# Softmax attention of the second block: nine projection units by seven block products each, their sums on VectorE

## What is computed

```python
def chunk_attention(u, w_in, b_in, rel_bias, w_out):
    q, k, v = jnp.split(u @ w_in + b_in, 3, axis=-1)     # u 256x1024, w_in 1024x3072
    ...                                                   # 16 heads of 64
        s = jnp.einsum('bhtd,bhjd->bhtj', qi, kb).astype(jnp.float32) + bias
        p = jax.nn.softmax(jnp.where(mb, s, NEG_INF), axis=-1).astype(vb.dtype)
        return jnp.einsum('bhtj,bhjd->bhtd', p, vb)
    ...
    return o @ w_out
...
    x = layer_norm_2(DEEPNORM_ALPHA * x + (1.0 + g1) * y, ln_g[i, 0], ln_b[i, 0])
```

## Time and profile before

| what | value |
|---|---|
| median of 3 runs | 1047.37 us (1047.06 to 1048.85) |
| the profiled execution, its own time | 1045.79 us |
| its span, first to last instruction | 1043.8 us |
| TensorE (PE) matmul busy | 1010.2 us, 97% |
| VectorE (DVE) busy | 652.4 us, 62% |
| ScalarE (ACT) busy | 203.1 us, 19% |
| mean granted TensorE clock | 0.992 |

### The profile page before, as it was taken

How to read it: one execution, slowest core, us unless ns; L and a number is a source line. 1 busy time by engine, 2 the same in 40 slices (tenths; PEclk the granted TensorE clock), 3 DMA queues, 4 the chain that set the end, 5 groups by cost and what they waited for, 6 DMA issues and landing times. The chain is left out here.

```text
span 1043.8 us, 12930 instructions
## 1 busy us (share of the span) xinstructions
PE 1010.2 (97%) x4878; PEld 712.5 (68%) x4880; DVE 652.4 (62%) x1533; ACT 203.1 (19%) x492; POOL 26.3 (3%) x53
## 2 busy tenths in 40 slices
PE   7999999999999999899999999999999999999994
PEld 4858755858755757656777777668886677777762
DVE  2786644785642341546899888975332577766668
ACT  4134214134212231202000000022223110001000
POOL 2000000000000000000001000001000000000000
PEclk9999999999999999999999999999999999999997
DMA  9954457754447355173669877825433345554411
GB/s 357 379 175 181 169 172 272 291 194 158 180 166 297 137 221 207 42 293 115 231 248 344 299 249 266 289 85 205 149 131 121 121 140 183 206 184 175 162 40 41
DMA packets 29909, 205.50 MB, mean 197 GB/s; under 512 B 3630, under 2 KB 3795, under 8 KB 6172
## 3 DMA queue, kind: packets, MB, share of 16 engines
q1 hardware_dynamic: 27116, 191.60, 50.4%
q0 software_dynamic: 2736, 13.11, 3.3%
HBM read 203.64 MB, written 1.05 MB: 196 GB/s over the span
## 5 line engine op out<-in xcount | busy, mean ns | idle before, releaser
L1503 PE MATMUL bank<-hT,raw 128*128 128x256 f32 x1056 | 235.1, 382 | 2.0 <-DMA raw<-units_dram 2.0
L1503 PEld LDWEIGHTS bank<-hT,raw 128*128 128x128 f32 x1056 | 200.1, 191 | 33.6 <-issue 3.8
L1792 PE MATMUL bank<-yT,arena 128*128 128x512 f32 x224 | 100.8, 593 | 0.0
L1792 PE MATMUL bank<-raw,arena 128*128 128x512 f32 x180 | 86.8, 593 | 0.0
L1792 PEld LDWEIGHTS bank<-yT,arena 128*128 128x128 f32 x224 | 42.5, 190 | 53.9 <-issue 51.7
L820 DVE CUSTOM_DVE_ANT_0 raw<-raw,crow 128x1024 f32<-128x1024 f32 x64 | 75.3, 1220 | 0.2 <-DVEq L118 0.2
L1816 PEld LDWEIGHTS bank<-hT,raw 128*128 128x128 f32 x448 | 54.3, 192 | 12.4 <-issue 12.4
L1513 PE MATMUL bank<-raw,hT 128*128 128x512 f32 x128 | 55.4, 592 | 0.0
L676 ACT ACTIVATE arena<-bank 128x512 f32<-128x512 f32 x28 | 16.7, 597 | 197.0 <-PE bank L1816 197.0
L1816 PE MATMUL bank<-hT,raw 128*128 128x128 f32 x448 | 54.5, 275 | 0.0
L1513 PE MATMUL bank<-raw,yT 128*128 128x512 f32 x112 | 49.5, 596 | 2.1 <-DVE yT L1432 2.0
(11 more groups left out here) (342 smaller groups left out, 1398.8 us busy)
## 6 DMA issues: line engine op xcount, KB each, us to landing
raw<-units_dram SPq DMA_DIRECT2D x180, 1024.0 KB, 4.8
arena<-ln_rows_dram POOLq DMA_DIRECT2D x4, 1024.0 KB, 5.5
arena<-att_line_dram POOLq DMA_DIRECT2D x4, 512.0 KB, 6.0
arena<-small_dram POOLq DMA_DIRECT2D x2, 896.0 KB, 7.1
arena<-ada_rows_dram POOLq DMA_DIRECT2D x1, 1536.0 KB, 8.0
xt<-x_dram SPq DMA_DIRECT2D x2, 512.0 KB, 4.5
arena<-post_g_dram POOLq DMA_DIRECT2D x2, 512.0 KB, 8.8
kst<-consts_dram SPq DMA_DIRECT2D x1, 608.0 KB, 15.9
```

The source lines that it names most:

```text
L1503: mm = pe.matmul(b[:, c * S:(c + 1) * S], raw[:, s, k * 256 + c * P:k * 256 + (c + 1) * P], act_t[:, k, :], start=(k == 0), stop=(k == KC ...
L1792: return pe.matmul(SB[i][:], x, y, start=False, stop=stop)
```

## The change

- The nine units of quads 1 to 3 are each multiplied as seven products of 128 x 512 by 512 x 128 blocks (`quad_unit`), four matmuls of 128 columns each, in place of 16 matmuls of 256 columns. Quad 0's units stay as they are.
- VectorE makes the four sums of tokens once (`token_sums`, in place of `x_rows(1)`), four sums of weights for each unit (`quad_weights`), and puts the seven products together straight from the banks in seven blocks (`quad_sums`, six instructions).
- TensorE waits in each unit: after two products for the weight sums (`asum_ready`), and after four for the drain of the unit before (`quad_drained`). The last quad waits for the ninth drain before the output projection.
- `keys` goes behind the head copies on ScalarE. The rows of x are made in quads 0 and 1, two pieces each, and `norm_rows(2)` goes behind the quads on GpSimd.

```diff
@@ gpsimd
             head_biases(0)
-            norm_rows(2)
             for qd in range(H - 1):
...
+            norm_rows(2)
             norm_rows(3)
@@ scalar, four_heads
                 head_exp(h0, 3, 1.0)
+                head_copy(h0, 2, (A[3], A[0]), True)
+                head_copy(h0, 3, (A[3], A[0]), True)
                 if more:
                     keys(qd + 1)
-                head_copy(h0, 2, (A[3], A[0]), True)
-                head_copy(h0, 3, (A[3], A[0]), True)
@@ vector
             stage_tiles(2)
-            x_rows(1)
+            token_sums(2, quad_tsum)
+            def quad_weights(u):
+                n = N_ATT + 3 + u
...
+                wait_landed(dve, 0, n)
+                if u >= 3:
+                    wait_used(dve, 0, n - 3)
+                ch.do(dve.tensor_tensor(d[:, 0], a[1][0], a[1][1], ALU.add))
+                ch.do(dve.tensor_tensor(d[:, 2], a[0][0], a[1][0], ALU.subtract))
+                ch.sync(1)
+                ch.do(dve.tensor_tensor(d[:, 1], d[:, 0], a[0][0], ALU.subtract))
+                ch.sync()
+                dve.tensor_tensor(d[:, 3], a[0][1], d[:, 1], ALU.subtract).then_inc(asum_ready, 1)
+            def quad_sums(u, c):
+                b = [x[:].rearrange("p (i n) -> p i n", i=4) for x in QUAD_BANKS[u % 3]]
+                wait_used(dve, 0, N_ATT + 3 + u)
+                ch.do(dve.tensor_copy(c[:, 6], b[0][:, 0]))
+                ch.sync()
+                ch.do(dve.tensor_tensor(c[:, 0:5:4], c[:, 6:7].to_broadcast([P, 2, P]), b[0][:, 1:3], ALU.add))
+                ch.sync()
+                ch.do(dve.tensor_tensor(c[:, 5], c[:, 4], b[0][:, 3], ALU.add))
+                ch.do(dve.tensor_tensor(c[:, 6], c[:, 4], b[1][:, 1], ALU.add))
+                ch.sync(1)
+                ch.do(dve.tensor_tensor(c[:, 2:4], c[:, 5:6].to_broadcast([P, 2, P]), b[1][:, 0:2], ALU.add))
+                ch.sync(1)
+                ch.do(dve.tensor_tensor(c[:, 1], c[:, 6], b[1][:, 2], ALU.add))
+                ch.sync()
+                dve.sem_inc(quad_drained, 1)
@@ vector, four_heads
                 scores_max(1)
                 head_norm(h0, 0)
                 head_norm(h0, 1)
+                if more:
+                    quad_sums(3 * qd, csum)
                 scores_max(2)
                 scores_max(3)
                 if more:
                     queries(qd + 1)
+                if qd < H - 2:
+                    quad_weights(3 * qd + 3)
                 head_norm(h0, 2)
                 head_norm(h0, 3)
+                if more:
+                    dve.wait_ge(ka_ready.sem, ka_ready.at(qd, 2))
+                    quad_sums(3 * qd + 1, prod)
+                if qd < H - 2:
+                    quad_weights(3 * qd + 4)
+                if qd < 2:
+                    x_piece(1, 2 * qd)
+                    x_piece(1, 2 * qd + 1)
+                if more:
+                    quad_sums(3 * qd + 2, csum)
                 dve.wait_ge(pv_ready.sem, h0 + H)
...
                 if more:
                     value_rows(qd + 1)
+                if qd < H - 2:
+                    quad_weights(3 * qd + 5)
             queries(0)
             gate_rows(1)
             value_rows(0)
+            for u in range(3):
+                quad_weights(u)
             for qd in range(H - 1):
                 four_heads(qd)
@@ tensor
+            def quad_unit(u):
...
+                a, b = asum[u % 3], QUAD_BANKS[u % 3]
...
+                wait_landed(pe, 0, n)
+                product(0, lambda k: w[:, k, 0:P], lambda k: hT[:, k, 0:P])
+                product(1, lambda k: w[:, 4 + k, 0:P], lambda k: hT[:, 4 + k, 0:P])
+                pe.wait_ge(quad_tsum, 1)
+                pe.wait_ge(asum_ready, u + 1)
+                product(2, lambda k: a[:, 1, k], lambda k: tsum[:, 1, k])
+                product(3, lambda k: a[:, 2, k], lambda k: tsum[:, 2, k])
+                if u > 0:
+                    pe.wait_ge(quad_drained, u)
+                product(4, lambda k: w[:, 4 + k, P:S], lambda k: tsum[:, 3, k])
+                product(5, lambda k: a[:, 0, k], lambda k: tsum[:, 0, k])
+                product(6, lambda k: a[:, 3, k], lambda k: hT[:, 4 + k, P:S]).then_inc(used[n % SLOTS], 1)
@@ tensor, four_heads (units 3qd, 3qd+1, 3qd+2 in the places of the three units before)
                 if more:
-                    unit_t(0, N_ATT + 3 * (qd + 1), hT, G[0])
+                    quad_unit(3 * qd)
                 else:
+                    pe.wait_ge(quad_drained, 9)
                     pe.wait_ge(oq_ready.sem, 2)
```

More of the change, by code:

```diff
@@ L369, in build @@
         v4_ready, oq_ready = event("v4_ready", 2), event("oq_ready", 1)
+        asum = [b.rearrange("p (i k n) -> p i k n", i=4, k=4) for b in (
+            arena[:, stay:stay + UNIT], gateT[:].rearrange("p a b -> p (a b)"), ytmp[:].rearrange("p a b -> p (a b)"))]
+        asum_ready, quad_tsum, quad_drained, pool_step = (sem(n) for n in ("asum_ready", "quad_tsum", "quad_drained", "pool_step"))
+        QUAD_BANKS = ((G[0], G[1]), (G[2], G[0]), (G[1], G[2]))
         def wait_landed(eng, turns, n):
@@ L746, in keys @@
                 act.wait_ge(bc_ready.sem, bc_ready.at(qd, 1))
-                wait_used(act, 0, N_ATT + 3 * qd + 1)
+                if qd == 0:
+                    wait_used(act, 0, N_ATT + 1)
+                    k = G[1][:]
+                else:
+                    act.wait_ge(quad_drained, 3 * qd - 1)
+                    k = prod[:, 0:4].rearrange("p i n -> p (i n)")
                 for c in range(2):
-                    act.activation(qk4[:, 1, c, :], G[1][:, c * S:(c + 1) * S], ACT.Identity, bias=bcur[:, 2 + c:3 + c],
+                    act.activation(qk4[:, 1, c, :], k[:, c * S:(c + 1) * S], ACT.Identity, bias=bcur[:, 2 + c:3 + c],
                                    scale=1.0).then_inc(ka_ready.sem, 1)
@@ L1242, in square, with token_sums @@
                 dve.tensor_tensor(hid[:, 0], relu[:], relu[:], ALU.mult).then_inc(hid_ready.sem, 1)
-            def token_sums(s):
+            def token_sums(s, told):
                 dve.wait_ge(us_act.sem, us_act.at(s, 12))
@@ L1253, in token_sums @@
                 ch.sync()
-                dve.tensor_tensor(tsum[:, 3], b[1][0], tsum[:, 1], ALU.subtract).then_inc(tsum_ready.sem, 1)
+                dve.tensor_tensor(tsum[:, 3], b[1][0], tsum[:, 1], ALU.subtract).then_inc(told, 1)
             def up_sums(n, g):
@@ L1345, in groups @@
                 step, lay = per // 3, s // 2
-                token_sums(s)
+                token_sums(s, tsum_ready.sem)
                 square(s)
@@ L1443, in _ @@
             stage_tiles(2)
-            x_rows(1)
+            token_sums(2, quad_tsum)
+            def quad_weights(u):
+                n = N_ATT + 3 + u
+                w = raw[:, n % SLOTS, :].rearrange("p (k n) -> p k n", k=KC)
+                a = [[w[:, 4 * k:4 * k + 4, c * P:(c + 1) * P] for k in range(2)] for c in range(2)]
+                d = asum[u % 3]
+                wait_landed(dve, 0, n)
[7 more added lines that the diff above has]
+                dve.tensor_tensor(d[:, 3], a[0][1], d[:, 1], ALU.subtract).then_inc(asum_ready, 1)
@@ L1446, in queries @@
             def queries(qd):
                 dve.wait_ge(bc_ready.sem, bc_ready.at(qd, 1))
-                wait_used(dve, 0, N_ATT + 3 * qd)
+                if qd == 0:
+                    wait_used(dve, 0, N_ATT)
+                    q = G[0][:]
+                else:
+                    q = csum[:, 0:4].rearrange("p i n -> p (i n)")
                 for c in range(2):
-                    dve.tensor_scalar(qk4[:, 0, c, :], G[0][:, c * S:(c + 1) * S], bcur[:, c:c + 1], HD_SCALE,
+                    dve.tensor_scalar(qk4[:, 0, c, :], q[:, c * S:(c + 1) * S], bcur[:, c:c + 1], HD_SCALE,
@@ L1454, in value_rows @@
                 dve.wait_ge(cur_ready.sem, cur_ready.at(qd, 2))
-                wait_used(dve, 0, N_ATT + 3 * qd + 2)
+                if qd == 0:
+                    wait_used(dve, 0, N_ATT + 2)
                 for t in range(NT):
-                    dve.tensor_tensor(v4[:, t, :], G[2][:, t * GW:(t + 1) * GW], vcur[:], ALU.add).then_inc(v4_ready.sem, 1)
+                    v = G[2][:, t * GW:(t + 1) * GW].rearrange("p (c n) -> p c n", c=2) if qd == 0 else csum[:, t:4:2]
+                    dve.tensor_tensor(v4[:, t, :].rearrange("p (c n) -> p c n", c=2), v,
+                                      vcur[:].rearrange("p (c n) -> p c n", c=2), ALU.add).then_inc(v4_ready.sem, 1)
             def four_heads(qd, more=True):
@@ L2005, in value_tile, with product @@
                     mm.then_inc(used[n % SLOTS], 1)
+            def quad_unit(u):
+                n = N_ATT + 3 + u
+                w = raw[:, n % SLOTS, :].rearrange("p (k n) -> p k n", k=KC)
+                a, b = asum[u % 3], QUAD_BANKS[u % 3]
+                def product(i, x, y):
+                    for k in range(4):
+                        l, r = (y(k), x(k)) if u % 3 == 2 else (x(k), y(k))
```

(9 more changed lines are left out.)

## The result

| | before | changed |
|---|---|---|
| median of 11 runs each | 1046.98 us | 1051.27 us |
| lowest to highest | 1044.4 to 1048.85 us | 1046.94 to 1053.2 us |
| the profiled execution | 1045.79 us | 1046.94 us |

The ratio of changed to before is 1.0047, 95% interval 1.0036 to 1.0058. It is slower by more than the 0.2% that the prediction took as its edge. A second series of the same kernel, 12 runs, had a median of 1050.2 us against 1046.79, ratio 1.0026 (1.001 to 1.0042), so its interval does not clear that edge. The ratios here are estimates of their own and not exactly the quotients of the two medians.

The account below looks back on a forecast made before the run. The prediction took TensorE alone to bound the kernel. Saving 6.66 us in nine units against 8.7 us of stalls and late turns gave +2.0 us, a median of 1049.4 us, range 1046.7 to 1052.8.

Parts of the forecast that it names:

- (a): Start of quad 0: TensorE stalls 0.81 us for the first weight sums and 3.79 us before the second turn.
- (b): From second turn to third and fourth, quads 0 and 1: 9.12 us on VectorE, a stall of 0.35 us each.
- (d): From the value unit's end to the next quad's second turn, before quads 1 and 2: stall of 1.28 us, twice.
- (c): From the fourth turn to the value unit's end: no stall, rows of x hidden with 0.1 us to spare.
- rival 2: Drains dearer through bank reads or semaphore steps, 2.44 us each: about +3.5 us, 1052.9 us at its end; chance 0.15.
- Rival 3: Not slower: the chain in (d) is 1.3 us shorter, quads 1 and 2 keep TensorE full; 1046.1 us, chance 0.15.
- Rival 4: Unit products take 0.95 us, giving 1052 us, or units take 6.13 us, giving 1048.6 us; chance 0.05.
- One sign of error: The prediction called itself wrong if TensorE is idle less than 1 us in quad 1.
- rival 1: TensorE's clock falls to half around the idling of (a) in quad 0; 1052.0 us, chance 0.15.
- the case that had 0.50: The prediction's own case, stalls outweighing the units' saving: 1048.3 to 1050.5 us, likeliest 1049.4, chance 0.50.

Follow-up runs that it names:

- e7: Changed kernel with the first three units' weight sums ahead of quad 0's value rows and all rows of x in quad 2; 1044.79 us, ratio 0.9981.
- a0: The changed kernel itself, unaltered, profiled once more; median 1050.2 us, ratio 1.0026 to the kernel before.
- e2: Changed kernel with twelve bf16 matmuls of zeros in TensorE's stall of quad 0, no wait removed; 1047.73 us, ratio 1.0019.
- e4: Changed kernel with the third unit's weight sums of quads 0 and 1 one stretch earlier and rows of x in quad 2; 1048.88 us, ratio 1.0019.
- e3: Kernel before with twelve unused VectorE sums between value rows and first row maxima of quad 0; 1053.65 us, ratio 1.0065.

## Why the prediction was right in sign and short in size

The measured ratio lies in the range, 1051.27 us in 1046.7 to 1052.8, and slower had the most weight. The step of 2.0 us was half of the measured 4.3.

**The sum of the waits held: +2.0 forecast, +2.24 measured** in the first profile, +2.21 with the filled stall. Term by term, from TensorE's timeline of that profile:

| term | forecast | measured |
|---|---|---|
| a unit of seven products | 6.27 | 6.35 |
| saved in nine units | 6.66 | 5.9 |
| (a) wait for the first weight sums | 0.81 | 0.96 |
| (a) wait before the second turn | 3.79 | 3.57 |
| (b) quads 0 and 1 | 0.35, 0.35 | 0.60, 0.34 |
| (d) before quads 1 and 2 | 1.28, 1.28 | 1.12, 1.13 |
| last quad, ninth drain | 0.53 | 0.36 |
| quads 0, 1, 2 | 28.5, 25.3, 24.9 | 28.92, 25.26, 24.93 |

The measured terms are differences of starts to what the order alone would give: two products at 1.79 us (717.94 - 715.19 - 1.79), a first turn at the unit's end and a second 0.30 us later (726.35 - 722.48 - 0.30). Two errors cancel in part: the units save 0.8 us less than forecast, and the waits are 0.6 us shorter. A unit costs 0.08 us more than seven times the net's product: the first two products behind the scores take 1.89 us (744.10 to 745.99) instead of 1.79, and a value unit's last is followed at 0.99 instead of 0.89 us (741.46 to 742.45). The waits sum to 8.08 us where I had 8.7. VectorE's single instructions were right to the hundredth: 2.54 us for the weight sums (715.18 to 717.72), and a drain's six instructions of 0.28 to 0.42 us each, as the SBUF rows had them:

```profile
742.55 0.29 DVE L1478 COPY arena<-bank 128x128 f32<-128x128 f32 x1
742.88 0.42 DVE L1480 TENSOR_TENSOR arena<-arena,bank 128x256 f32<-128x256 f32 x1
...
744.07 0.28 DVE L1487 TENSOR_TENSOR arena<-arena,bank 128x128 f32<-128x128 f32 x1
744.50 0.69 DVE L1543 TENSOR_SCALAR yT<-bank 128x512 f32<-128x512 f32 x1
```

From the copy to the next work it is 1.95 us, 0.11 more than summed. In (c) it is 2.01 us (735.57 to 737.58), and in (b) 2.12 us (726.21 to 728.33), because VectorE first waits for its own last sum or semaphore step (idle for 0.21 and 0.33 us in its rows). So rival 2 was right in sign, but the drains are 0.11 to 0.28 us dearer and not 0.6. The Trainium skill's longer fixed term for reads from PSUM ("VectorE: DVE Perf Modes", section on the TRN2 errata) did not show in additions here, 0.42 us for 256 columns from either memory. For an operation on one tensor there was a difference: `queries` (L1499, 128 x 256) takes 475 to 484 ns from the bank and 345 to 489 ns, median 416, from SBUF.

**(b) beside GpSimd** held in the one row: 1.53 us for the one weight sum under its copies (730.88), 1.52 forecast. The whole of (b) came out by errors that cancel in quad 1 (9.09 us where 9.12 was summed: drain 2.11 for 1.84, maxima and queries 2.29 for 2.44, sums 3.38 for 3.37, norms 1.31 for 1.47), and in quad 0, where maxima and queries took 2.55 us, they did not: 0.60 us of wait for 0.35. **(c)** held: e7 shows the rows of x hidden. **Rival 3** is out: (d) cost 1.12 and 1.13 us. Rival 4 is out but for the 0.08 us. One sign of error needs care: TensorE idle for less than 1 us in quad 1. The busy column gives 0.82 us (25.26 less 24.44), but a busy matmul's end is modelled; by the starts of the rows TensorE waits 0.34 + 1.12 us there.

**What failed is the weight and the reading of rival 1**, the clock. Its mechanism and price were there: 1052.0 us as one case, with 0.15. It is, as far as the mean clocks tell, the usual case: ten of the first eleven runs have 0.986 to 0.988 and nine of the next twelve 0.986 to 0.989, where none of the twelve filled ones is under 0.990. The fall costs 1.96 and 0.95 us in the two profiles of it and 2.5 us between the medians of a0 and e2, where I had 2.6. That price was also read loosely: the first matmuls' 634 ns were taken for half clock, but the granted clock of that stretch is 1.00 in the trace, so those rows do not show it. What shows it is a0, where the first two products took 2.71 us instead of 1.88. I argued that the rows showed a fall only behind the last matmul. That was too little reading. The trace of the kernel before has falls inside it, in stretches that the prediction did not take in, such as this one:

```profile
355.00:360.00 5.00, 5.00 (x19) 4.18 (x18) 2.87 (x5) 2.07 (x2) 0.00 (x0) 0.77 0.01 5
```

No wait of TensorE in that trace is longer than 2.1 us. A fall behind a stall of 3 us, with two short turns in it, should have been the more likely case of the two. The likeliest forecast would then have been 1052.0 us. That the measured median lies inside the range is owed to that rival, which the range took in, and not to the case that had 0.50. Why the first profile had the same stall and no fall stays open.

## What to carry to other kernels

Work that is to run on an engine with free time must be placed where the time is free: here 7.6 us of sums stood behind a wait during which the engine had idled 7 us, and moving one line was worth 6.9 us by the medians. Follow each engine from wait to wait in its fixed order and not by its busy share: VectorE's total was nearly TensorE's, yet its order decided over 2.2 us more. Price a stall of TensorE twice, once as the wait and once for the clock that may fall with it, and look at the granted clock of the whole trace before giving that case its chance.

## What the runs showed of the hardware

- A stall of TensorE of 2.8 to 3.1 us was followed by a fall of the granted clock from 2.4 to 1.2 GHz in three of four traces, at the stall's end (a0), or 1.8 to 1.9 us later, behind the turns (e4, e3). The clock stayed low for 3.4 us (e3, e4) or 6.8 us (a0). In the fourth it did not fall: the same kernel had quad 0 in 28.92 and in 30.88 us.
- Matmuls of bf16 zeros into a free bank, 2.5 us of them, kept the granted clock at 1.00 through quad 0; the median was 2.5 us lower (0.7 us by the ratios).
- The kernel before varies by 9 us from run to run (1041.37 to 1050.14 us in 29 runs) with its mean clock (0.995 to 0.988): falls elsewhere in the program (at 350 to 360 and 425 to 430 us in its trace), which no experiment here touched.
- An addition of 128 x 512 from two SBUF operands took 1.53 us beside GpSimd's copies (730.88 to 732.33 us in the changed kernel; a copy of 128 x 1024 runs there from 730.76 for 1.10 us) and 0.68 us without.
